# A two-model transformer kernel: latents split earlier and into other tiles, sums of squares one projection later, loop buffers cleared elsewhere, last norm by tokens

## The chip, the cores and the metric

One core of one Trainium2 chip runs the whole program in one launch. The metric is the time on the device, in microseconds (us), as the median of the runs. The engines are called PE (matrix multiplication; its weight loads are listed as PEld), DVE (vector), ACT (activation functions), POOL, and SP, which only issues DMA transfers here.

## The reference, cut to what matters

The input is one sequence of 256 tokens of width 2048, in float32. Three layers follow one another.

1. Layer A: a modulated RMS norm, a wide projection, sparse attention beside a pooled branch, an output projection, and then a mixture of 32 experts. Each token goes to two experts of one group.
2. Layer B ("even"): a norm, a projection, a gated linear recurrence beside sliding-window attention, and an output projection (`wb` in the kernel).
3. Layer C ("odd"): a norm and a projection into latents and differential attention heads; the latents are normed and projected up to queries, keys and values; an output projection (`wc`) and a last norm close it.

```python
def odd_layer(h, w_in, q_norm, w_uq, kv_norm, w_ukv, ..., subln, w_out):
    z = h @ w_in
    c_q, c_kv, k_rope, mla_gate, dq, dk, dv, diff_gate = split_cols(z, ODD_SPLITS)   # c_q is 768 wide, c_kv 512
    q = (rmsnorm_2(c_q, q_norm) @ w_uq).reshape(B, S, MLA_HEADS, MLA_NOPE + MLA_ROPE)
    ...
# after each even and odd layer: x = x + layer(rmsnorm_2(x, gain)); at the end: rmsnorm_2(x, final_norm_gain)
```

## The kernel before

**Layout.** The residual stream `X` lies in SBUF as 16 chunks of 128 features by 256 tokens: features on the partitions, tokens along the row. A norm over features is therefore a sum over partitions, made by PE as a product with a matrix of ones.

**Products in three terms.** Each float32 operand of a projection is split into a rounded high part (type fp32r) and the rest. A projection adds high x high, high x low and low x high. Weights arrive by DMA in half units of 128 x 1024 (`land`). ACT makes the high part `WH` (step `hi`, L1636), DVE the low part `WL` (step `lo`, L1945), and PE multiplies (L1185). Four slots hold `WH` and `WL`, so the `hi` of a half waits until PE has used the half four places back. A projection of one chunk of 128 outputs is two halves of 24 matmuls each.

**Order.** Every engine works through its own list in order, written out beforehand by two functions, `order_a` (layer A up to the routing) and `order_bc` (everything behind the expert loop). `Order.proj` appends the halves of one projection to PE's list, its evacuation to ACT's, and the next weights' `hi` and `lo` to ACT's and DVE's. Steps that follow a projection are put on `lagged` and come one or more projections later. A step waits with `needs(engine, step)` until another engine's counter has passed a step. An engine that waits holds up all that stands behind in its list.

**The routing and the loop.** Layer A ends with the routing: `top`, `place` (slot numbers of the tokens), `before` (a list of expert numbers), `pick` (a one-hot matrix for the first tile of 32 tokens), `list` (the number of tiles and the expert of each, cast to integers for SP), `weights`. Then the first tile's tokens are gathered by PE (L1432), copied by ACT (L1777), turned by PE (L1440) and scaled and shifted by DVE (`inputs`, L2361 and L2365, which make `XG`). A loop over the tiles follows. One tile takes 12 MB of expert weights in 12 slots of `ring`; SP reloads a slot when PE has used it (`w_used`, L1043). The first 12 slots are loaded ahead of the loop (L1030). The vector engine clears the loop's buffers: four of them inside `pick` (L2237 to L2240), and four more behind the routing (L2369 to L2372). `weigh` (L2344 to L2350) makes the scatter weights.

**Behind the loop.** After `wb`, layer C projects `cq` (6 chunks), `ckv` (4), `kr`, `dk`, `dq`, `dv`, `dg` and `mg`. The squares of the last `wb` chunk are added on DVE (`sqsum`, L2109) and summed over the partitions by PE (`ss`, L1291); the norm's factor is applied later to the products. The latents `cq` and `ckv` are split into high and low parts by the steps `ch` (ACT, L1678) and `cl` (DVE, L1969), in ten chunks, after the last `mg` projection, because their target `HH`/`HL` holds the layer's input until then. `silu mg` (L1684) and the evacuations of the up-projections `qr` stand behind them in ACT's list.

**The end.** After the last `wc` chunk: ACT evacuates it, DVE adds it to `X` (L2100), ACT squares, DVE sums (L2109), PE sums over the partitions into all 128 of them (L1291), DVE scales (L1920), ACT takes the root (L1701), DVE the reciprocal of 128 x 256 values (L2152), and DVE multiplies each of the 16 chunks by gain and factor (L2163); SP writes four groups out.

## Time and profile before

| | |
|---|---|
| median of 3 runs | 2349.46 us (2347.33 to 2351.78) |
| profiled execution, its own time | 2358.7 us |
| its span, first to last instruction | 2356.9 us |
| PE busy | 2089.4 us (89%) |
| mean DMA rate | 295 GB/s |

The time of the profiled execution is 1.8 us more than its span and 9.2 us more than the median of the timed runs. The page cuts the span into 40 slices of 58.9 us. Slices 1 to 9 are layer A, 10 to 24 the loop over the tiles, 25 to 40 the layers B and C. In the timeline, a row has its start, the time that it spans, the engine, the line, the operation, what it writes and reads, and behind that in brackets the idle time of the engine before it and what ended it.

### The profile page before, as it was taken

To read this page: it belongs to the slowest core of one execution; us is meant where nothing else is said; L and a number is where in the kernel's file an instruction comes from. 1 tells how busy PE (TensorE), PEld (TensorE's weight loads), DVE (VectorE), ACT (ScalarE), POOL (GpSimd) and SP (SyncE) were. 2 spreads that over 40 slices of the span, in tenths; PEclk is the share of its full clock that TensorE was granted. 3 is DMA by queue.
4 is the path that set the end of the run, shared out by engine and by line. 5 is a ranking of instruction groups with operands and counts; after the bars stand their busy time and mean duration, and the time that the engine had idled before them with its cause. 6 is when DMAs were issued, how large, how long until landed. Compare 5 with 4: busy or idle time off the path is not lost.

```text
span 2356.9 us, 38440 instructions
## 1 busy us (share of the span) xinstructions
PE 2089.4 (89%) x14538; PEld 1364.2 (58%) x14538; DVE 1252.0 (53%) x2281; ACT 858.9 (36%) x1312; POOL 55.2 (2%) x56
## 2 busy tenths in 40 slices
PE   6899998989988888888888888999999999997997
PEld 2677766762222222222222222998889999997887
DVE  3455567545444444444444445558866454577655
ACT  3333344431111111111111113457855444565543
POOL 0000000000000000000000001011100010010000
PEclk9999999999999999999999999999999999998998
DMA  9998987899999999999999999463445455542442
GB/s 368 354 348 291 310 285 233 299 350 364 427 428 428 428 427 427 427 428 428 428 427 427 427 428 372 166 208 121 134 152 182 153 177 182 175 147 88 135 134 91
DMA packets 135047, 695.43 MB, mean 295 GB/s; under 512 B 14992, under 2 KB 15120, under 8 KB 85264
## 3 DMA queue, kind: packets, MB, share of 16 engines
q1 hardware_dynamic: 134928, 693.79, 76.7%
q8 instruction: 81, 1.33, 0.2%
q14 instruction: 38, 0.31, 0.0%
HBM read 691.63 MB, written 2.10 MB: 294 GB/s over the span
## 4 chain that ended last, share of the span: by engine, by line
PE 49%; DMA 34%; DVE 8%; ACT 4%; SPq 3%; issue 2%; DVEq 0%; ACTq 0%
PE acc L1185 34%; DMA ring<-in_w 30%; DMA land<-in_stream_a 3%; PE psO L1237 3%; PE psS L1468 3%; PE acc L1182 3%; DVE WL L1945 2%; SPq L1043 2%; ACT WH L1636 1%; DMA land<-in_stream_bc 1%; PE psM L1454 1%; PE acc L1454 1%; PE psT L1119 1%; ACT SB L1722 0%; PE psO L1127 0%
## 5 line engine op out<-in xcount | busy, mean ns | idle before, releaser
L1185 PE MATMUL acc<-HH,WH 128*128 128x256 f32 x2152 | 633.8, 295 | 11.8 <-DVE HL L1969 5.4
L1945 DVE TENSOR_TENSOR WL<-land,WH 128x1024 fp32r<-128x1024 f32 (+2 forms) x346 | 417.4, 1208 | 417.7 <-ACT WH L1636 413.6
L1185 PE MATMUL acc<-HH,WL 128*128 128x256 f32 x2152 | 616.0, 286 | 0.0
L1185 PE MATMUL acc<-HL,WH 128*128 128x256 f32 x2152 | 615.2, 286 | 0.0
L1636 ACT ACTIVATE WH<-land 128x1024 fp32r<-128x1024 f32 (+2 forms) x350 | 362.4, 1037 | 222.3 <-PE acc L1185 176.8
L1185 PEld LDWEIGHTS acc<-HH,WH 128*128 128x128 f32 x2152 | 420.5, 195 | 34.6 <-issue 11.6
L1185 PEld LDWEIGHTS acc<-HH,WL 128*128 128x128 f32 x2152 | 420.6, 195 | 2.0 <-issue 1.0
L1185 PEld LDWEIGHTS acc<-HL,WH 128*128 128x128 f32 x2152 | 419.9, 195 | 0.0
L1468 PE MATMUL psS<-ring,low 128*32 128x512 f32 x2048 | 273.9, 607 | 105.3 <-DMA ring<-in_w 100.8
L1468 PEld LDWEIGHTS psS<-ring,low 128*32 128x32 f32 x2048 | 40.8, 108 | 316.4 <-DMA ring<-in_w 285.0
L2355 DVE TENSOR_TENSOR X<-acc,X 128x512 f32<-128x512 f32 x128 | 88.6, 692 | 218.9 <-PE acc L1454 218.9
L1787 ACT ACT_TABLE_LOAD x32 | 41.1, 1283 | 447.1 <-PE psS L1468 447.1
L2355 DVE TENSOR_TENSOR X<-psM,X 128x512 f32<-128x512 f32 x128 | 88.6, 692 | 210.0 <-PE psM L1454 210.0
L1492 PE MATMUL psO<-ring,SB 128*32 128x512 f32 x1024 | 122.3, 598 | 42.9 <-DVE SB L2389 35.8
L1454 PE MATMUL psM<-low 128*128 128x512 f32 x264 | 150.4, 652 | 4.9 <-DVE low L2377 2.3
L1454 PE MATMUL acc<-low 128*128 128x512 f32 x264 | 149.3, 647 | 1.4 <-DVE X L2096 1.4
L1787 ACT ACTIVATE low<-psS 128x512 f32<-128x512 f32 x64 | 38.2, 597 | 244.6 <-PE psS L1468 244.2
L1237 PE MATMUL psO<-land,high_a 128*32 128x512 f32 x672 | 96.1, 648 | 35.2 <-DMA land<-in_stream_a 34.4
L1454 PEld LDWEIGHTS psM<-low 128*128 128x128 f32 x264 | 39.7, 189 | 116.6 <-DVE X L2355 80.5
L1454 PEld LDWEIGHTS acc<-low 128*128 128x128 f32 x264 | 39.5, 188 | 112.4 <-DVE X L2355 107.6
L1185 PE MATMUL acc<-lowR,WH 128*128 128x256 f32 x512 | 95.4, 289 | 5.8 <-DVE lowR L1964 5.8
L1492 PEld LDWEIGHTS psO<-ring,SB 128*32 128x32 f32 x1024 | 27.1, 109 | 116.6 <-DVE SB L2389 43.4
(370 smaller groups left out, 2413.4 us busy)
## 6 DMA issues: line engine op xcount, KB each, us to landing
ring<-in_w SPq DMA_DIRECT2D x384, 1024.0 KB, 26.0
land<-in_stream_a SPq DMA_DIRECT2D x284, 512.0 KB, 7.6
land<-in_stream_bc SPq DMA_DIRECT2D x246, 512.0 KB, 4.0
land<-in_stream_bc SPq DMA_DIRECT2D x12, 384.0 KB, 3.5
X<-in_xT SPq DMA_DIRECT2D x1, 2048.0 KB, 14.0
out<-low SPq DMA_DIRECT2D x4, 512.0 KB, 2.6
cst<-in_const SPq DMA_DIRECT2D x1, 1514.5 KB, 9.6
low<-in_w_pool SPq DMA_DIRECT2D x1, 1024.0 KB, 8.3
```

Source lines behind the costliest of these rows:

```text
L1043: sp.dma_start(ring[:, s, :], src[bass.ds(e, 1), s % 4, :, :].rearrange("e p n -> (e p) n")).then_inc(tile_in[s], 16)
L1119: mm = pe.transpose(psT[:, kt, h, :], SB[:, n % 2, h, P * kt:P * kt + P], ident)
L1182: mm = pe.matmul(bank[:, S * tt:S * tt + S], h[rows[kk]][:, P * tt:P * tt + P], w[:, kk, :], start=(z == 0 and i == 0 and tt == 0), stop=s ...
L1185: mm = pe.matmul(bank[:, 0:S], w[:, kk, :], h[rows[kk]], start=(z == 0 and i == 0), stop=stop)
L1237: mm = pe.matmul(bank[CAP * c:CAP * c + CAP, :], cB[:, 4 * q + c, :], w[c // 2][:, c % 2, :], start=(q == 0), stop=(q == 3), tile_position ...
L1454: return pe.matmul(ybank[m % 2], OE[:, P * c:P * c + P], SJ[:, 2 * half:2 * half + 2, :], start=True, stop=True)
L1468: mm = pe.matmul(bH[s // 4][CAP * c:CAP * c + CAP, :], XG[:, k % 4, k // 4, :], ring[:, s, 512 * c:512 * c + 512], start=(s % 4 == 0), sto ...
L1492: mm = pe.matmul(bW2[CAP * c:CAP * c + CAP, :], AT[:, s - 8, :], ring[:, s, 512 * c:512 * c + 512], start=(s == 8), stop=(s == 11), tile_p ...
L1636: ins = act.activation(wh, src, ACT.Copy)
L1787: act.activation(HS[:, b, :], bankS[b], ACT.Copy).then_inc(moe["h_copied"], 1)
L1945: ins = dve.tensor_tensor(wl, src, wh, ALU.subtract)
L2355: dve.tensor_tensor(moe_out(m), ybank[m % 2].rearrange("p (a s) -> p a s", a=2), moe_out(m), ALU.add)\
```

## The change

It has four parts.

1. **Latents.** `ch` and `cl` of the ten latent chunks move from behind `mg` to behind the first ten projections of `dk` and `dq`, one chunk a projection. The high parts go to the columns of tables that no step reads any more (cosines, sines and rotation matrices of layer A, in `cst`) and to free chunks; the low parts overwrite the latents themselves (`latent_split`).
2. **Squares.** `ss` of the last `wb` chunk comes one projection later on PE, and so do the sums of the `cq` chunks.
3. **Start of the loop.** The clears move into two steps, `clear 0` (behind ACT's copy of the gate rows, within the last `wo` projections) and `clear 1` (between `top` and `place`). `pick` comes directly behind `place`, ahead of the list of experts, the gather becomes a step of PE's list, and `weigh` for the first tile comes ahead of `list`. PE's ten filler products become nine. Within the loop `pick` waits for ACT's copy of the gathered tokens (`g_copied`), no longer for PE's gather.
4. **Last norm.** DVE adds the last `wc` chunk straight from PSUM. The sum of squares is taken by tokens (a column of two values a partition, four products on PE), root and reciprocal work on 128 x 2 values, and two products spread the factor over all partitions into PSUM (`rwide`). ACT multiplies each `X` chunk by the gain during the `wc` projections (`gx`, 16 of them), and DVE then multiplies by the factor from PSUM in five operations (`FINAL`).

```diff
+LAST_OUT = ("wc", KD - 1)
+FINAL = ((0, 4), (4, 4), (8, 4), (12, 2), (14, 2))
 def evac_by(x):
-    return "dve" if x[0] in ("bk", "p") else "act"
+    return "dve" if x[0] in ("bk", "p") or x == LAST_OUT else "act"
...
             if x[0] != "wp":
                 self.add("act", "sq", x)
+            if x[0] == "wc":
+                self.add("act", "gx", x[1])
...
-        if x[1] == KD - 1:
+        if x == ("wb", KD - 1):
+            self.lagged.append((1, self.sum_squares, x))
+        elif x[1] == KD - 1 or x == ("wc", KD - 2):
             self.sum_squares(x)
...
             o.add("act", "gt2rows")
+            o.add("dve", "clear", 0)
...
+    o.add("dve", "clear", 1)
     o.add("dve", "place")
     o.add("pe", "keep_busy")
-    o.add("dve", "before")
+    o.add("dve", "pick")
+    o.add("pe", "gather")
     o.add("pe", "beforeT")
     o.misc.append(("beforeT",))
-    o.add("dve", "pick")
+    o.add("dve", "weights")
     o.add("dve", "list")
-    o.add("dve", "weights")
...
         o.proj(("cq", n))
-        o.lagged.append((1, o.sum_squares, ("cq", n)))
+        o.lagged.append((2, o.sum_squares, ("cq", n)))
...
-    for n in range(8):
-        o.proj(("dk", n))
-    for n in range(8):
-        o.proj(("dq", n))
+    latent = [("cq", c) for c in range(6)] + [("ckv", c) for c in range(4)]
+    for x in [(name, n) for name in ("dk", "dq") for n in range(8)]:
+        o.proj(x)
+        if latent:
+            z = latent.pop(0)
+            o.add("act", "ch", *z)
+            o.add("dve", "cl", *z)
...
-    for name, n in (("cq", 6), ("ckv", 4)):
-        for c in range(n):
-            o.add("act", "ch", name, c)
-            o.add("dve", "cl", name, c)
     o.add("act", "silu", "mg", 0, 8)
...
+        def latent_split(name, c):
+
+            hi = {"cq": (0, 1, 2, 3, 60, 61), "ckv": (62, 63, 51, None)}[name][c]
+            hi = rotR[:, :] if hi is None else cosR[:, hi, :] if hi < 4 else highR[:, hi - 48, :]
+            at = (cCQ if name == "cq" else cCKV) + c
+            return hi, lowR[:, at, :] if at < 48 else highR[:, at - 48, :]
...
                 if not first:
-                    dve.wait_ge(moe["g_full"], i)
+                    dve.wait_ge(moe["g_copied"], i)
...
+                    elif what == "gx":
+                        n = step[1]
+                        needs("dve", *(("evac", LAST_OUT) if n == KD - 1 else ("res", ("wc", n))))
+                        ins = act.activation(W(MIX + n)[:, 0, :], X[:, n, :], ACT.Copy, scale=C("gain_f", n, 1))
...
+                        if step[1] == "wc":
+                            then(dve.reciprocal(rtok, rsum))
+                            for tt in range(NT):
+                                ins = dve.tensor_scalar(RT[:, P * tt:P * tt + P], ident, rtok[:, tt:tt + 1], None, ALU.mult)
...
-                        g = C("gain_f")
-                        for c in range(4 * step[1], 4 * step[1] + 4):
-                            ins = dve.scalar_tensor_tensor(out=W(MIX + c)[:, 0, :], in0=X[:, c, :], scalar=g[:, c:c + 1],
-                                                           in1=RT, op0=ALU.mult, op1=ALU.mult)
+                        z = W(MIX + c, n)
+                        ins = dve.tensor_tensor(z, z, psM[:, None, 0:S].to_broadcast([P, n, S]), ALU.mult)
```

**How the instructions move.** Three places follow, rows of the built programs; they hold no times. The first is DVE's list from the end of `place` (the reduction into `small`) to the first operation of the loop. `sti` holds the list for SP, `psO` and `low` are loop buffers. Before:

```order
L2233 TENSOR_REDUCE small<-high_a 128x2 x2
...
L2235 COPY SB<-cst 128x128
...
L1821 TENSOR_TENSOR SB<-SB 128x64
...
L2247 CAST sti<-psM 1x48
L2205 TENSOR_REDUCE high_a<-high_a 128x2
...
L2332 TENSOR_LOAD sti
L2332 ISA x2
L2369 MEMSET psO 128x512
L2370 MEMSET low 128x512
...
L2361 TENSOR_TENSOR low<-acc,small 128x512
L2365 TENSOR_TENSOR low<-low,ada 128x512
```

And after:

```order
L2289 TENSOR_REDUCE small<-high_a 128x2 x2
L1862 TENSOR_SCALAR SB<-SB,small 128x32
...
L1866 TENSOR_TENSOR SB<-SB 128x64
L2305 TENSOR_SCALAR high_a<-high_a,cst 128x32
...
L2410 TENSOR_SCALAR SB<-SB 128x128
L2310 CAST sti<-high_a 1x1
L2311 CAST sti<-psM 1x48
L2421 TENSOR_TENSOR low<-acc,small 128x512
L2425 TENSOR_TENSOR low<-low,ada 128x512
L2432 TENSOR_LOAD sti
```

The five operations of `pick` now stand directly behind `place`, the clears are gone from here, and DVE reads the number of tiles (TENSOR_LOAD) behind `XG` and not ahead of it.

The second place is ACT's list around the last `mg` evacuation (L1596, in the change L1637), with `exp` of a softmax (L1722, L1765) ahead and `silu mg` behind. Before:

```order
L1722 ACTIVATE SB,small<-SB,small 128x256 x4
L1678 ACTIVATE HH_54<-low 128x256 x8
L1678 ACTIVATE HH_54<-high_bc 128x256 x2
L1684 ACT_TABLE_LOAD
L1684 ACTIVATE low<-low 128x2048
```

And after:

```order
L1637 ACTIVATE low<-acc 128x256
L1677 ACTIVATE WH_50<-land_58 128x1024
...
L1765 ACTIVATE SB,small<-SB,small 128x256 x4
L1677 ACTIVATE WH_50<-land_58 128x1024
L1723 ACT_TABLE_LOAD
L1723 ACTIVATE low<-low 128x2048
```

The ten copies of the latents between `exp` and the table load of `silu` are gone from this place.

The third place is the end of DVE's list. Before:

```order
L2100 TENSOR_TENSOR X<-X,high_bc 128x256
L2109 TENSOR_TENSOR high_bc<-high_bc 128x256 x2
L1920 TENSOR_SCALAR high_bc<-psM 128x256
L2152 RECIPROCAL high_bc<-high_bc 128x256
L2163 SCALAR_TENSOR_TENSOR low<-X,col,high_bc 128x256 x16
```

And after:

```order
L2192 TENSOR_TENSOR X<-X,acc 128x256
L2153 TENSOR_TENSOR high_bc<-high_bc 128x256
L2160 TENSOR_SCALAR small<-psM 128x2
L2203 RECIPROCAL small<-small 128x2
L2205 TENSOR_SCALAR high_bc<-cst,small 128x128 x2
L2221 TENSOR_TENSOR low<-low,psM 128x1024 x3
L2221 TENSOR_TENSOR low<-low,psM 128x512 x2
```

The operations on 128 x 256 values between the sum and the last products are replaced by ones on 128 x 2 and 128 x 128, and 16 last products by five larger ones.

## Rows read from the trace of the kernel before

**Rows 1.** The page: the DMA rate of the 40 slices.

```profile
GB/s 368 354 348 291 310 285 233 299 350 364 427 428 428 428 427 427 427 428 428 428 427 427 427 428 372 166 208 121 134 152 182 153 177 182 175 147 88 135 134 91
```

**Rows 2.** Windows: span, busy time of the engines, PE's clock, DMA share, GB/s.

```profile
530.00:535.00 5.00, 2.63 (x9) 0.71 (x10) 3.68 (x11) 0.00 (x0) 0.00 (x0) 0.52 0.12 51
...
620.00:640.00 20.00, 18.32 (x122) 5.40 (x120) 11.23 (x27) 3.06 (x5) 0.00 (x0) 1.00 1.01 428
```

**Rows 3.** Timeline of DVE, from the end of `place` to `XG`.

```profile
522.39 0.24 DVE L2242 TENSOR_SCALAR high_a<-high_a,cst 128x32 f32<-128x32 f32 x1
...
523.15 0.30 DVE L1817 TENSOR_SCALAR SB<-SB,small 128x32 f32<-128x32 f32 x1
...
524.11 0.23 DVE L1821 TENSOR_TENSOR SB<-SB 128x64 f32<-128x64 f32 x1
...
525.00 0.18 DVE L2247 CAST sti<-psM 1x48 int32<-1x48 f32 x1
...
526.02 0.16 DVE L2209 TENSOR_TENSOR small<-small,high_a 128x2 f32<-128x2 f32 x1
527.36 0.48 DVE L2369 MEMSET psO<- 128x512 f32 x1 [1.18 <-issue]
...
529.16 0.17 DVE L2344 TENSOR_SCALAR SB<-SB,small 128x128 f32<-128x128 f32 x1
...
530.72 0.68 DVE L2361 TENSOR_TENSOR low<-acc,small 128x512 f32<-128x512 f32 x1
```

**Rows 4.** Timeline of PE and of SP's queue at the loop's start.

```profile
524.48 1.92 PE L1432 MATMUL acc<-low,SB 128*32 128x512 f32 x16 [0.63 <-DVE SB L1821]
527.17 0.66 PE L1440 MATMUL acc<-cst,low 128*128 128x128 f32 x4 [0.77 <-ACT low L1777]
532.37 1.94 PE L1468 MATMUL psS<-ring,low 128*32 128x512 f32 x8 [4.54 <-DVE low L2365]
...
534.50 26.26 SPq L1043 DMA_DIRECT2D ring<-in_w  x12
```

**Rows 5.** Timeline of DVE and PE around the last squares of `wb`.

```profile
1823.23 1.22 DVE L1945 TENSOR_TENSOR WL<-land,WH 128x1024 fp32r<-128x1024 f32 x1 [0.70 <-ACT WH L1636]
...
1825.06 1.19 PE L1291 MATMUL psM<-high_bc,ones 128*128 128x256 f32 x2 [4.20 <-DVE high_bc L2109]
...
1826.26 0.41 PE L1185 MATMUL acc<-HH,WL 128*128 128x256 f32 x1
...
1833.82 0.59 PE L1291 MATMUL psM<-high_bc,ones 128*128 128x256 f32 x2
```

**Rows 6.** Timeline of ACT, DVE and PE behind the last `mg`.

```profile
2143.16 3.55 ACT L1678 ACTIVATE HH<-low 128x256 fp32r<-128x256 f32 x8
...
2147.62 1.28 ACT L1684 ACT_TABLE_LOAD   x1
...
2152.23 0.96 DVE L1945 TENSOR_TENSOR WL<-land,WH 128x768 fp32r<-128x768 f32 x1 [3.99 <-ACT WH L1636]
...
2156.40 1.11 PE L1119 MATMUL psT<-cst,SB 128*128 128x128 f32 x4 [4.62 <-DVE SB L1893]
```

**Rows 7.** Timeline of ACT, PE and DVE at the end of the program.

```profile
2340.84 0.38 ACT L1578 ACTIVATE high_bc<-acc 128x256 f32<-128x256 f32 x1 [2.97 <-issue]
...
2342.92 1.19 PE L1291 MATMUL psM<-high_bc,ones 128*128 128x256 f32 x2 [2.17 <-DVE high_bc L2109]
...
2345.26 1.75 DVE L2152 RECIPROCAL high_bc<-high_bc 128x256 f32<-128x256 f32 x1 [0.61 <-ACT high_bc L1701]
2347.05 6.80 DVE L2163 SCALAR_TENSOR_TENSOR low<-X,col,high_bc 128x256 f32<-128x256 f32 x16
```

**Rows 8.** Page group of a PSUM-fed DVE addition; ACT's timeline during `dk` and `wc`.

```profile
L2355 DVE TENSOR_TENSOR X<-acc,X 128x512 f32<-128x512 f32 x128 | 88.6, 692 | 218.9 <-PE acc L1454 218.9
...
1912.40 1.06 ACT L1636 ACTIVATE WH<-land 128x1024 fp32r<-128x1024 f32 x1 [1.39 <-PE acc L1185]
...
2320.68 1.06 ACT L1636 ACTIVATE WH<-land 128x1024 fp32r<-128x1024 f32 x1 [0.38 <-PE acc L1185]
```

More of the change, by code:

```diff
@@ L785, in order_bc @@
     o.add("dve", "rstd", "wc")
-    for g in range(4):
+    o.add("pe", "rwide")
+    for g in range(len(FINAL)):
         o.add("dve", "final", g)
@@ L1162, in product @@
                     HH, HL = ([z[:, c, :] for c in range(KD)] for z in (HH0, HL0))
+                elif name in ("qn", "qr", "kn", "vm"):
+                    HH, HL = ([latent_split(*z)[i] for z in [("cq", c) for c in range(6)] + [("ckv", c) for c in range(4)]]
+                              for i in range(2))
                 else:
@@ L1280, in run @@
                                            start=False, stop=True, skip_group_check=True)
+                    elif what == "ss" and step[1][0] == "wc":
+                        x = step[1]
+                        first = x != LAST_OUT
+                        if first:
+                            misc_free(("ssum", "wc"))
+                            needs(k, "dve", o, "sqsum", x)
+                            sq = W(dSA)[:, 0, :]
+                        else:
+                            needs(k, "act", o, "sq", x)
+                            sq = W(dSQ + x[1] % 2)[:, 0, :]
+                        for tt in range(NT):
+                            mm = pe.matmul(psM[:, tt:tt + 1], sq[:, P * tt:P * tt + P], ones[:, 0:1],
+                                           start=(first and tt == 0), stop=not first, skip_group_check=True)
+                    elif what == "rwide":
+                        needs(k, "dve", o, "rstd", "wc")
+                        for tt in range(NT):
+                            mm = pe.matmul(psM[:, P * tt:P * tt + P], ones[:, :], W(dRT)[:, 0, P * tt:P * tt + P], start=True, stop=True)
                     elif what == "ss":
@@ L1374, in run @@
                     elif what == "keep_busy":
-                        for _ in range(10):
+                        for _ in range(9):
                             mm = pe.matmul(bankS[1][:, 0:S], ones[:, :], X[:, 0, :], start=True, stop=True)
+                    elif what == "gather":
+                        needs(k, "act", o, "evac", ("h2t", (1, 3)))
+                        mm = gather(0)
                     elif what == "beforeT":
                         misc_free(step)
-                        needs(k, "dve", o, "before")
+                        needs(k, "dve", o, "pick")
                         mm = pe.matmul(psM[0:1, 0:48], eid[:, 0:1], ident[:, 0:48], start=True, stop=True)
@@ L1773, in copy_gather @@
             def copy_gather(i, first=False):
-                act.wait_ge(moe["g_full"], i + 1)
-                if not first:
+                if first:
+                    act.wait_ge(done[0]["pe"], A.at["pe"][("gather",)])
+                else:
+                    act.wait_ge(moe["g_full"], i)
                     act.wait_ge(moe["gt_full"], i)
@@ L2233, in run @@
                             ins = dve.tensor_reduce(pos_w[:, 2 * kk:2 * kk + 2], tmp2[:, kk], AX.X, ALU.add)
-                    elif what == "pick":
+                    elif what == "clear" and step[1] == 0:
+                        needs("act", "gt2rows")
                         dve.tensor_copy(J, K("slot")).then_inc(moe["j_ready"], 1)
-                        pick(0, True)
                         dve.memset(AT, 0.0).then_inc(moe["at_ready"], 1)
@@ L2327, in run @@
                     count += 1
-            dve.wait_ge(table_in, 32)
-            run(0, A)
-            dve.wait_ge(done[0]["dve"], len(A.steps["dve"]))
-            tiles = dve.value_load(sti[0:1, 48:49], min_val=1, max_val=MAX_TILES)
             OE = W(mOE, 2).rearrange("p a s -> p (a s)")
```

141 lines of the change are left out of this document (79 added, 62 removed).

## The prediction

> **What bounds the kernel now.** First the page's slices [rows 1]: in slices 12 to 24 the DMA rate stands at 427 to 428 GB/s. That is the loop, and its time is the bytes of the expert weights; PE waits there. A change can shorten it only by letting the stream start earlier. In layers A, B and C the rate is far below that, and PE is nearly always busy, so there the waits of PE count one for one. I then listed PE's idle times and read what ended each. Four places touch the change: ahead of the loop [rows 3, 4], at the last squares of `wb` [rows 5], behind the last `mg` [rows 6], and the end [rows 7]. Nothing else in this kernel moves.
>
> **1. Start of the loop.** The first 12 slots are full soon after 530 us: from there to 535 the DMA share is 0.12 [rows 2]. The next transfer is issued at 534.50, when PE's first group of expert products, begun at 532.37, has released a slot [rows 4]. PE waited 4.54 us for `XG` there. The chain after the change, hop by hop:
> - `place` ends just ahead of 522.39, where the list of experts starts; `pick` starts 0.76 us later at 523.15 [rows 3]. It now takes that place, so all of `pick`, gather, copy and turn come 0.76 earlier: the gather at 523.72, the turned tiles at 527.17 + 0.66 - 0.76 = 527.07 [rows 4].
> - What else DVE must have done by then: `pick` 1.19 (523.15 to 524.34), the expert list 0.5 at most (it fits into the 0.76 with a copy of 0.23), `weights` 1.00 (525.18 to 526.18), `weigh` 1.56 (529.16 to 530.72), and the casts 0.3: from 522.39 to 526.94. That is just ahead of 527.07, so neither is much of a wait for the other.
> - `XG` starts at 527.2, and PE 1.65 later (530.72 to 532.37): 528.85. The gain is 532.37 - 528.85 = 3.5 us. The clears (527.36 to 529.16 with the reading of the tile count ahead of them, 1.18) have left this chain [rows 3]. They cost nothing if their new places are idle: seven small operations before the last two `wo` chunks, where I read DVE idle for 4.7 us ahead of the next addition, and two in DVE's wait for PE between `top` and `place`. Without that cover they cost their 1.8 and 0.8 us.
> - The first eight products take 1.94 us after that wait, against about 1.06 in full loop tiles, and the granted clock of the stretch is 0.52, the lower of the two levels (1.2 against 2.4 GHz) [rows 2, 4]. PE's idle time before them shrinks from 4.54 to 1.8 us. If the clock then stays high, the slot is free 0.9 us sooner still: 4.4. I take 3.8; the ends are 0 and 4.4.
>
> The Trainium skill, "TensorE: Matmul & The Clock Gate", section "HAM oscillation", says that waits between bursts of products bring the low clock back, so that each burst starts slow. By that rule a shorter wait is the way to keep it; the sum would be 0.6 us larger. The trace agrees on the slow restart, at 0.52.
>
> **2. Squares.** PE finishes `cq` 0 at about 1820.7 and stands until 1825.06 (4.20 idle), because the addition of the last squares stands on DVE behind a `lo` that ends at 1824.45 [rows 5]. Then `cq` 1 runs at 0.213 us a product instead of 0.12 (0.41 long each instead of 0.28) and is done at 1833.82 [rows 5]. One projection later the sum is ready: `cq` 1 runs straight on, 1820.7 + 48 x 0.12 = 1826.5, and the squares follow in 0.25. The point that was reached at 1833.8 is reached at 1826.7: 7.1 us. The weights for it are there: `WL` for `cq` 2 is complete at 1824.45 [rows 5], and the next `hi` needs only the half that ends at 1823.6. What comes late next: the sum over `cq` 0 must wait for DVE to have read the `wb` sum; that read stands behind two more `lo` and ends at about 1830.6, `cq` 2 at 1832.5. Lower bound 4.2 (the wait alone), upper 7.5.
>
> **3. Latents.** Here the wait named on PE misleads. PE waits 5.4 us for the first latent part, but if that wait alone goes, PE runs one up-projection and a second and then waits for the transposes at 2156.40 [rows 6], and these wait on ACT. The chain: ten latent copies (2143.16 to 2147.61), table load, `silu mg`, evacuation, `hi`, then DVE's `lo` at 2152.23, for which DVE stood 3.99 us [rows 6], then normalising and scaling (4.1 us), then the transposes at 2156.40. Without the ten copies the table load follows `exp` at once, at 2143.16, and every later link comes 2147.62 - 2143.16 = 4.46 us earlier. PE waits at the transposes instead, some 8 us, and restarts there at the low clock as it does now. So the gain is 4.5 and not 5.4 plus the slow products of the first projection. In `dk` and `dq` the ten copies cost ACT 0.44 us a projection, where it has 1.39 idle ahead of its second `hi` alone, and DVE the same, with more [rows 8]. A `hi` ends 2.4 us with its `lo` behind it and is read three halves later (8.6 us). Ends 3.5 and 6.
>
> **4. The end.** Old chain: PE done 2340.75, evacuation, addition, squares, sum, and the last 16 products start at 2347.05 and end at 2353.85 [rows 7]. New chain, from the same instant:
> - DVE adds from PSUM at 2340.87, 0.43; then the sum of the squares of chunk 14 stands on DVE, to 2341.76; four small products on PE for each of two sums, 0.55 each: 2343.0.
> - Three operations on 128 x 2, 0.17 to 0.2 each with 0.1 between engines: 2343.8. Two of 128 x 128 on DVE, 0.5: 2344.35.
> - `rwide` on PE: 0.6 at the high clock, 1.2 at the low one, by the two levels at which the squares ran [rows 5, 7]: 2345.0 to 2345.6.
> - The last products: PSUM-fed 128 x 512 takes 0.69 [rows 8]. Eight of these would be 5.5; three are doubled, and one start saved in each makes it about 5.3. End 2350.6, against 2353.85: 3.2. The 1.75 us of the wide reciprocal [rows 7] are the main part.
> - The last transfer is half as large (256 KB against 512 KB), about 0.6 us at 428 GB/s [rows 1]; I count 0.4.
>
> Together 3.6, ends 2 and 4.5. The 16 `gx` on ACT cost about 0.5 each in `wc`, where ACT's idle time before the second `hi` is 0.38 [rows 8]: that `hi` starts 0.1 late and has 6 us to spare.
>
> The Trainium skill speaks against this part. "VectorE: DVE Perf Modes", section "The TRN2 errata", gives an operation that reads PSUM about twice the fixed cost of one that reads SBUF. By its table, an estimate, the old 16 products would take 5.2 us and the new five 4.9. The trace has 6.80 for the old ones, so the measurement decides.
>
> **Sum.** 3.8 + 7.1 + 4.5 + 3.6 = 19.0 us. Against the profiled execution (2358.7, of them 2356.9 span) that is 2339.7; against the median 2349.46, which is 9.2 below it, 2330.5. The four waits lie on the chain in either, so I forecast 2330.5.
>
> **The rivals.**
> - *Start of the loop gives nothing.* The stream runs until slots run out: if the new order frees the later slots no sooner, or SP's reading of the list (now 1.5 us later) holds the first transfer, only 15.2 remain: 2334.3. For it: from 535 to 560 the rate is still under 428. Against: every slot is released by the same PE list, which shifts as a whole. Chance 0.1.
> - *The squares' wait only moves.* If the `wb` sum is read later than `cq` 2 ends, PE stops one projection later and restarts slowly again. Half of the 7.1 is left: 2334.0. My margin is 1.9 us. Chance 0.08.
> - *PE's first wait was the bound in the latents, and the transposes come early too.* Then 5.4 and the slow products (18 x 0.09) go, 7.0 in all: 2328.0. Against: DVE's 3.99 us wait on ACT [rows 6]. Chance 0.06.
> - *ACT falls behind.* 26 additional operations of 0.5, if none found idle time, give back 13 us: 2343.5. Against: [rows 8]. Chance 0.05.
> - *Slower.* `pick` in the loop now waits for ACT's copy, 0.8 us behind the gather. If DVE were on the chain of each tile, 32 x 0.8 = 25.6 us would be added: 2356.1. It decides once more than 0.6 us a tile gets through. Against: the loop runs at 428 GB/s [rows 1, 2], and that copy belongs to the tile before. Chance 0.02.
> - *No change within 0.2%.* The program does what it says by its order of instructions; only several failures of the above would leave less than 4.7 us. Chance 0.02.
>
> My forecast has the rest, 0.67. 0.2% is 4.7 us, about what a measurement of this kernel can tell from no change. Faster: all but the last two cases and part of the ACT case, 0.95; same 0.03; slower 0.02. The range takes the ends of the parts, not all at one side: 0 to 4.4, 4.2 to 7.5, 3.5 to 6 and 2 to 4.5 give 12.5 to 21 if two fall short, with some room for the spread of medians: 2325.5 to 2337.5. This takes in the first three rivals.
>
> **What would show it.** The first expert product near 528.9 and SP's first reload near 530 to 531; no idle time of PE at the last squares, and `cq` 1 at 0.12 a product; no PE wait ahead of the first `qr`, but one of some 8 us ahead of the transposes of the last differential job, 4.5 us earlier relative to the end of `mg`; the last multiplication some 10 us behind PE's last projection, against 13.1 now. I am wrong if the loop's end moves by less than its start, if PE shows a new wait between `cq` 1 and `ckv`, or if `WH` in `wc` comes late.

## The result, and the profile after

The changed kernel took 2329.29 us (median of 4 runs, 2328.52 to 2330.41), the kernel before 2348.60 (4 runs): 19.3 us less. The ratio is 0.9925, with a 95% interval of 0.9910 to 0.9939, which is 14.3 to 21.1 us. The forecast was 2330.5, of them 19.0 us gained.

Whoever subtracts the two profiled spans gets another number, 2356.9 - 2327.9 = 29.0 us. The profiled execution of before was 9.2 us above its timed runs, and that of the changed kernel 1.1 above its own. So the rows shown ahead of the prediction hold some 9 us that a usual execution does not have. Where they lie is the first experiment.

**Start of the loop.** Timelines of PE, DVE and SP's queue of the changed kernel; they answer to [rows 3, 4].

```profile
519.92 0.30 DVE L1862 TENSOR_SCALAR SB<-SB,small 128x32 f32<-128x32 f32 x1
520.87 0.23 DVE L1866 TENSOR_TENSOR SB<-SB 128x64 f32<-128x64 f32 x1
521.25 1.92 PE L1096 MATMUL acc<-low,SB 128*32 128x512 f32 x16 [0.45 <-DVE SB L1866]
523.94 0.66 PE L1104 MATMUL acc<-cst,low 128*128 128x128 f32 x4 [0.73 <-ACT low L1822]
524.32 0.18 DVE L2311 CAST sti<-psM 1x48 int32<-1x48 f32 x1
524.63 0.69 DVE L2421 TENSOR_TENSOR low<-acc,small 128x512 f32<-128x512 f32 x1
526.28 1.06 PE L1509 MATMUL psS<-ring,low 128*32 128x512 f32 x8 [1.69 <-DVE low L2425]
528.36 1.06 PE L1509 MATMUL psS<-ring,low 128*32 128x512 f32 x8
530.41 1.06 PE L1509 MATMUL psS<-ring,low 128*32 128x512 f32 x8
527.55 31.84 SPq L1065 DMA_DIRECT2D ring<-in_w  x16
```

`pick` starts where `place` ends, `XG` begins at 524.63, right behind the turned tiles (523.94 + 0.66), and PE waits 1.69 us instead of 4.54. The whole profile is 2.5 us earlier here than that of before; *route* in the table below differs by more than that between executions of equal code. Counted from the copy that opens `place` (516.93 now, 519.42 before), the first expert product comes at 9.35 us instead of 12.95: 3.6 earlier, where I had 3.5. The first eight take 1.06 us and not 1.94. SP reloads the first slot 10.62 us after that copy (527.55) and not 15.08 (534.50), 4.5 sooner.

**Squares and latents.** PE's timeline at the last squares of `wb` [rows 5], then DVE, ACT and PE behind the last `mg` [rows 6].

```profile
1816.49 0.28 PE L1250 MATMUL acc<-HL,WH 128*128 128x256 f32 x1
1816.62 0.59 PE L1373 MATMUL psM<-high_bc,ones 128*128 128x256 f32 x2
1819.97 0.42 DVE L2166 TENSOR_SCALAR high_bc<-psM 128x256 f32<-128x256 f32 x1
1822.80 0.59 PE L1373 MATMUL psM<-high_bc,ones 128*128 128x256 f32 x2
...
2126.43 1.28 ACT L1723 ACT_TABLE_LOAD   x1
2131.03 0.96 DVE L1990 TENSOR_TENSOR WL<-land,WH 128x768 fp32r<-128x768 f32 x1 [5.57 <-ACT WH L1677]
2135.20 1.12 PE L1181 MATMUL psT<-cst,SB 128*128 128x128 f32 x4 [7.50 <-DVE SB L1938]
```

The wait ahead of the first up-projection in the kernel before, which has no counterpart now:

```profile
2144.24 0.55 PE L1185 MATMUL acc<-HH,WH 128*128 128x256 f32 x1 [5.44 <-DVE HL L1969]
```

PE goes straight from a projection into the squares, with no idle time. DVE has read the sum of `wb` by 1820.39, 2.4 us before PE overwrites it at 1822.80, so no wait has taken the old one's place. In the latents, the wait of 5.44 us that stood ahead of the first up-projection is gone, and one of 7.50 us stands ahead of the transposes: the forecast had some 8.

**The end.** Timeline of PE, DVE and SP's queue; it answers to [rows 7].

```profile
2316.35 1.02 PE L1357 MATMUL psM<-ones,high_bc 128*128 128x1 f32 x8 [1.13 <-DVE high_bc L2153]
2318.24 0.48 DVE L2205 TENSOR_SCALAR high_bc<-cst,small 128x128 f32<-128x128 f32 x2
2318.78 0.71 PE L1362 MATMUL psM<-high_bc,ones 128*128 128x128 f32 x4 [1.40 <-DVE high_bc L2205]
2319.60 5.17 DVE L2221 TENSOR_TENSOR low<-low,psM 128x1024 f32<-128x1024 f32 x5 [0.87 <-PE psM L1362]
2320.85 4.29 SPq L1072 DMA_DIRECT2D out<-low  x5
```

PE's last projection ended at 2315.22 (2316.35 less the 1.13 idle) and the last multiplication at 2324.77, 9.55 us later; the forecast was 9.9. From there to the end of the span it is 3.13 us, against 3.05 before. The last transfer is half as large, and that gained nothing.

### The profile page after: what moved, and what is told of

Its sections match the earlier page's. It is cut to its first block, busy times and chain, and to the rows that moved or that the text cites. A ratio compares the mean times of both kernels' runs of the same rounds, so it can differ in the third digit from the quotient of the medians.

```text
span 2327.9 us, 38446 instructions
## 1 busy us (share of the span) xinstructions
PE 2076.3 (89%) x14546; PEld 1354.5 (58%) x14546; DVE 1249.1 (54%) x2271; ACT 866.4 (37%) x1327; POOL 55.2 (2%) x56
## 4 chain that ended last, share of the span: by engine, by line
PE 50%; DMA 34%; DVE 7%; ACT 3%; SPq 3%; issue 2%; DVEq 0%; ACTq 0%
PE acc L1250 35%; DMA ring<-in_w 30%; DMA land<-in_stream_a 4%; PE psO L1302 3%; PE acc L1247 3%; PE psS L1509 3%; DVE WL L1990 2%; SPq L1065 2%; ACT WH L1677 1%; DMA land<-in_stream_bc 1%; PE acc L1118 1%; PE psM L1118 1%; PE psT L1181 1%; PE psO L1195 0%; PE psO L1189 0%
## 5 line engine op out<-in xcount | busy, mean ns | idle before, releaser
L1250 PE MATMUL acc<-HH,WH 128*128 128x256 f32 x2048 | 598.6, 292 | 6.4 <-DVE HL L2009 4.1
L1250 PE MATMUL acc<-HH,WL 128*128 128x256 f32 x2048 | 583.2, 285 | 0.0
L1250 PE MATMUL acc<-HL,WH 128*128 128x256 f32 x2048 | 583.0, 285 | 0.0
L1250 PEld LDWEIGHTS acc<-HH,WH 128*128 128x128 f32 x2048 | 397.0, 194 | 28.0 <-issue 11.6
L1250 PEld LDWEIGHTS acc<-HH,WL 128*128 128x128 f32 x2048 | 397.1, 194 | 1.7 <-issue 1.0
L1250 PEld LDWEIGHTS acc<-HL,WH 128*128 128x128 f32 x2048 | 396.6, 194 | 0.0
L1250 PE MATMUL acc<-lowR,WH 128*128 128x256 f32 x600 | 119.8, 287 | 5.8 <-DVE lowR L2009 5.8
L1250 PEld LDWEIGHTS acc<-lowR,WH 128*128 128x128 f32 x600 | 98.2, 194 | 6.8 <-ACT lowR L1712 4.3
```

The costliest lines, as they stand in the source:

```text
L1250: mm = pe.matmul(bank[:, 0:S], w[:, kk, :], h[rows[kk]], start=(z == 0 and i == 0), stop=stop)
```

## The experiments

All kernels of a group ran beside the kernel before. The summary over all 14 profiles comes first, since each experiment draws on it. Each profile is cut at the same events; the stretches are differences of start times, in us:

- *route*: to the copy that opens `place`. *loop*: from there to the first transfer of the weights behind the loop. *B*: to the last product of `cq` 0. *sq*: to the first product of `cq` 2. *C1*: to the second of the four long reciprocals (128x512) of layer C. *lat*: to the third. *r*: to the fourth. *C2*: to the end of the last projection. *tail*: to the end of the last multiplication.

```
                     route    loop      B     sq     C1    lat      r     C2   tail
before              519.42  917.13 384.03  13.48 294.04  29.27  23.39 159.99  13.10
before_again        517.32  916.81 380.69  12.57 294.04  29.27  21.17 158.15  12.57
only_squares        520.46  917.02 383.79   6.12 294.52  29.27  22.68 156.52  12.58
only_latents        519.46  916.50 380.47  12.57 294.05  24.80  23.42 158.14  12.57
only_start          521.84  912.71 381.38  12.56 294.05  29.28  21.18 156.37  12.57
only_norm           515.54  917.02 383.37  12.51 294.04  29.27  21.18 155.04   9.56
the changed kernel  516.93  910.31 383.50   6.12 294.52  24.80  21.14 157.90   9.55
after_again         517.77  911.72 383.30   6.12 294.53  24.79  21.15 157.84   9.55
after_no_squares    512.33  911.46 381.50  12.53 294.05  24.79  22.68 157.75  10.08
after_fill          518.85  911.07 383.54   6.12 294.52  24.79  21.16 157.70  10.06
after_silu          515.92  914.49 383.52   6.13 294.51  21.58  21.16 161.35   9.56
after_silu_dve      519.29  910.85 383.22   6.13 294.52  19.73  23.44 158.08   9.64
after_reorder       513.46  913.02 383.69   6.12 294.52  20.50  23.67 158.39   9.55
after_reorder_fill  515.12  912.07 381.16   6.13 294.52  20.51  23.66 160.27   9.56
```

Three columns are nearly constant wherever the code is the same (*sq*, *C1*, *lat*), and four move by 2 to 10 us between executions of equal code (*route*, *B*, *r*, *C2*). What is read from the first kind is exact to tenths, but for the *sq* of the first profile of before; a whole time is not.

### before_again: where the surplus of the first profile lies

The kernel before, without an edit.

> The kernel before, unchanged: a control, and a second profile of it. The profiled execution of before took 2358.7 us, 9.2 us more than its timed runs; that of the changed kernel took 2330.4, 1.1 more than the median of its runs. Theory 1 (chance of the execution): the surplus sits in stretches that ran at a low PE clock behind a wait, 2170 to 2180 us with a granted clock of 0.70 and 0.62 above all, and a second profile shows another set of them, so its span comes out between 2345 and 2352. Theory 2 (the recording itself costs it): the second profile has again a span near 2357 and the same slow stretches. Ratio to before 1.000 in either.

Measured: 1.0002 (0.9989 to 1.0016), its span 2345.6. Theory 1 holds, with a span inside its 2345 to 2352: the second profile is 11.3 us shorter, by 2.1 in *route*, 3.3 in *B*, 0.9 in *sq*, 2.2 in *r*, 1.8 in *C2* and 0.5 in *tail*. What differs is PE's clock, wherever it was looked up: in *sq* and *r* below, in the tail, and at one place in *B* (see what stays open). *route*, *C2* and the rest of *B* were not traced to it. A window in the stretch *r* and PE's row at its wait, first of the first profile and then, the same place 6.7 us earlier, of the second; the number ahead of the DMA share is the granted clock.

```profile
2170.00:2180.00 10.00, 8.36 (x38) 7.36 (x39) 3.66 (x7) 2.67 (x4) 0.00 (x0) 0.66 0.22 74
2172.76 1.22 PE L1335 MATMUL psM<-high_bc,cst 128*128 128x256 f32 x2 [1.53 <-DVE high_bc L2315]
```

```profile
2163.30:2173.30 10.00, 8.34 (x60) 7.46 (x61) 5.84 (x8) 4.20 (x6) 0.00 (x0) 1.00 0.28 85
2166.09 0.70 PE L1335 MATMUL psM<-high_bc,cst 128*128 128x256 f32 x2 [1.53 <-DVE high_bc L2315]
```

The wait is 1.53 us in both, but around it one execution ran at 0.66 and the other at full speed, and the same two products took 1.22 and 0.70. The tail shows it in one row: the sum of the last squares [rows 7] takes 1.19 us in the first profile, and in the second this.

```profile
2332.19 0.67 PE L1291 MATMUL psM<-high_bc,ones 128*128 128x256 f32 x2 [2.17 <-DVE high_bc L2109]
```

1.19 - 0.67 = 0.52 is the whole difference of the two tails (13.10 and 12.57). After a wait of 2.17 us in both, the products came out at either level.

### only_squares and after_no_squares: the second part alone, and left out

The first is before with these lines, the second the changed kernel without them:

```diff
-        if x[1] == KD - 1:
+        if x == ("wb", KD - 1):
+            self.lagged.append((1, self.sum_squares, x))
+        elif x[1] == KD - 1:
...
-        o.lagged.append((1, o.sum_squares, ("cq", n)))
-        if n == 0:
+        o.lagged.append((2, o.sum_squares, ("cq", n)))
+        if n == 1:
```

> Before with the second part of the change alone: the squares of the last wb chunk and those of the cq chunks come one projection later. My step: the wait of 4.20 us and the slow cq 1 behind it go, 7.1 us in all, about 2341.5, with cq 1 at 0.12 us a product. Rival 1, the wait alone goes and the products stay slow: 4.2 us. Rival 2, the wait moves one projection on: 3.6 us, with a new idle time of PE ahead of the sum over cq 0.

> The changed kernel with the second part undone (the squares of the last wb chunk one projection earlier again). From cq 0's last product to the first of cq 2 it took 13.48 us in the first profile of before, 12.57 in the second, and 6.13 in the changed kernel. Theory: undone, it costs 6.4 us, near 2337. Rival 1 (the parts alone and together differ, since a wait of 4.2 us is a place where something else can catch up): less than 5. Rival 2 (my own 7.1): only where the low clock lasts as long as in the first profile.

Measured: 0.9976 (0.9960 to 0.9992), 5.6 us, for the part alone. Without it the changed kernel stood at 0.9946 (0.9933 to 0.9958) where it has 0.9925 and 0.9926 in two measurements: 4.8 us. In the stretch *sq* it is sharp: 6.12 or 6.13 in all eight profiles with the part and 12.51 to 12.57 in five of the six without it; only the first profile of before had 13.48. The difference is 6.4, and 0.48 comes back in *C1* (294.52 against 294.04), where the two products of the sum over `cq` 0 now lie, so 6.0. The wait and the slow restart both go, as in my step, so it is not the wait alone (rival 1 of the first expectation); rival 2 is out too, since none of the eight profiles with the part has a new wait: PE's first idle time behind these squares is one of 0.40 us, 26 us on, and the kernels without the part have the same one with 0.36. The 4.8 us of the timed runs lie under the 5 that rival 1 of the second expectation set, but their interval does not tell 4.8 from 6.0; the stretch does. My 7.1 was taken from the one execution in which the low clock lasted longest. Windows of before_again show the shorter dip behind the same wait:

```profile
1814.00:1819.00 5.00, 1.10 (x10) 0.89 (x8) 4.19 (x5) 2.59 (x4) 0.00 (x0) 1.00 0.53 178
1819.00:1824.00 5.00, 4.64 (x24) 4.55 (x25) 0.93 (x3) 0.42 (x1) 0.00 (x0) 0.66 0.50 162
```

### only_latents: the first part alone

The edit is that of the diff shown ahead: `ch` and `cl` go behind the projections of `dk` and `dq`, with `latent_split`.

> Before with the first part of the change alone: the ten latent chunks are split behind the first ten projections of dk and dq. My step: the chain over ACT gives 4.5 us, about 2344.1. Rival: 7.0 to 7.4 us, about 2341.5. The two profiles speak for both: between the last mg and the transposes of the last differential job the changed kernel gained 4.47 us, and between there and the first queries of the next jobs another 2.9, because before ran 10 us there at a granted clock of 0.70 and 0.62 and the changed kernel at 1.00. If those 2.9 belong to the change, the profile here shows 1.00 in that stretch and the time falls by 7.4; if they are chance of one execution, timed runs show 4.5.

Measured: 0.9982 (0.9970 to 0.9993), 4.2 us. The stretch *lat* is 24.80 against 29.27: 4.47, and my step had 4.46. The rival's other 2.9 us were chance: *r* is 23.42 here, as long as in the first profile of before. *C1*, in which the ten splits now lie, is 294.05 against 294.04. They cost nothing there.

### only_start: the third part alone

The edits of the diff ahead in `order_a`, `pick`, `clear`, the gather step and the wait on `g_copied`; nothing behind the loop.

> Before with the third part of the change alone: the start of the loop. My step: 3.8 us, of them 3.5 on the chain to XG, about 2344.8. Rival (clock): the two profiles show 6.9 us between the first load of the ring and the end of the loop: 3.7 up to the first expert product, and the rest because the first expert products, the first two additional products behind them and the second eight run at the high clock instead of 0.52 and 0.80; then about 2341.7. Rival (ACT in the loop): if the copy that pick now waits for counted, the time would be 2370 or so, 0.8 us a tile more.

Measured: 0.9979 (0.9965 to 0.9993), 4.9 us. In *loop*, five profiles without the part have 916.50 to 917.13, seven with it and without a filler 910.31 to 914.49, in the mean 912.1: 4.8 us, in single executions 2.4 to 6.6. ACT's copy is on no chain in the loop, or *loop* would be 25 longer. Most of why the gain varies is seen in PE's timelines: first the start alone, then after_again, both with the wait of 1.69 us that the changed kernel has.

```profile
531.18 1.94 PE L1469 MATMUL psS<-ring,low 128*32 128x512 f32 x8 [1.69 <-DVE low L2371]
533.04 1.76 PE L1098 MATMUL psM<-low 128*128 128x512 f32 x2
534.74 1.07 PE L1469 MATMUL psS<-ring,low 128*32 128x512 f32 x8
```

```profile
527.11 1.93 PE L1509 MATMUL psS<-ring,low 128*32 128x512 f32 x8 [1.69 <-DVE low L2425]
528.98 1.71 PE L1118 MATMUL psM<-low 128*128 128x512 f32 x2
530.62 1.06 PE L1509 MATMUL psS<-ring,low 128*32 128x512 f32 x8
```

The same wait, and the first eight products take 1.94 and 1.93 here but 1.06 in the changed kernel's first profile. The second group of eight starts 3.5 or 3.6 us behind the first there, and 2.1 in the changed kernel: 1.5 us lost. In before, 4.54 us of idle time stood ahead, and the third group was slow to start as well:

```profile
536.24 1.42 PE L1468 MATMUL psS<-ring,low 128*32 128x512 f32 x8
538.64 1.06 PE L1468 MATMUL psS<-ring,low 128*32 128x512 f32 x8
```

538.64 is 6.27 us behind the first product at 532.37 [rows 4]; in the changed kernel it is 4.13 (526.28 to 530.41). Read so in all twelve profiles without a filler, *loop* falls into three pieces. From the copy that opens `place` to the first expert product it is 12.93 to 13.04 us in the five without the part and 9.34 or 9.35 in the seven with it: 3.6. From there to the third group it is 6.27 to 6.85 in the five, and in the seven 4.13 three times, 5.56, 5.61, 5.70 and 7.04 (after_silu, where the second group ran slow as well): in the mean 6.6 against 5.2, so 1.4. The rest is 896.8 to 898.1 in all twelve. So the clock behind the wait makes up to 2.9 us of the spread, and 1.3 are of that rest.

### after_fill: filler products in that wait

```diff
             gather_t(0)
+            for _ in range(7):
+                pe.matmul(bankS[1][:, 0:S], ones[:, :], X[:, 0, :], start=True, stop=True)
             needs(0, "dve", A, "list")
```

> The changed kernel with seven filler products (128x256, about 0.22 us each at the high clock, 1.6 us in all) on PE between the turning of the gathered tokens and the first expert product, where PE waits 1.69 us. So far the first expert products ran at the low clock in two of four profiles with that wait (1.93 us for the first eight) and at the high one in the two others (1.06). Theory (PE's idle time ahead of the products decides): with 0.1 us of idle left they run at 1.06 in every execution, and the time is 1 to 1.5 us below after_again in the mean, with a smaller spread. Rival: the clock falls for another reason (the waits of 0.4 and 0.7 us ahead of it, or the light load of the filler itself); then the filler runs at half speed too, ends 1.5 us late, and the time is 1 to 1.5 us above.

Measured: 0.9931 (0.9918 to 0.9944), not below the changed kernel's 0.9925. Timeline of PE:

```profile
526.34 3.19 PE L1501 MATMUL psS<-X,ones 128*128 128x256 f32 x14
529.46 1.07 PE L1511 MATMUL psS<-ring,low 128*32 128x512 f32 x8
```

I had mispriced the filler. The trace writes two rows for one such product, so that 0.22 us is half of one: seven took 3.19 us at the high clock and not 1.6, and put the first expert product 1.3 us late. The products behind it did run at the high clock, here and in after_reorder_fill, but that the filler was the reason is not shown, since without it some executions have it too.

### only_norm: the fourth part alone

The edits of the diff ahead in `evac_by`, `FINAL`, `gx`, the token sums, `rstd`, `rwide` and `final`.

> Before with the fourth part of the change alone: the last norm by tokens. My step: 3.6 us. By the profiles of before: the last multiplication ended 13.10 us after PE's last projection in the first profile, but 12.57 in the second and in those of three single parts; in the changed kernel it ended 9.55 after. So I now expect 3.0 us, about 2345.3, and 9.55 in the profile here. Rival (smaller last transfer counts too): 0.4 us more between the last multiplication and the end of the span; the profiles of before and after speak against it with 3.05 and 3.13 there. Rival (ACT falls behind by gx): the projections of wc take longer than in before, and nothing is gained.

Measured: 0.9986 (0.9969 to 1.0003), 3.3 us, with an interval that reaches no change. The profile decides: *tail* is 9.56 against 12.57 or 12.58 in four profiles without the part, 3.0 us. (The 10.06 and 10.08 of two other kernels are `rwide` at the low clock, 1.22 us in after_fill instead of 0.71.) *C2*, in which the 15 first `gx` run on ACT, is 155.04, no longer than elsewhere.

### after_again: do the parts add up?

The changed kernel, without an edit.

> The changed kernel, unchanged: a second profile and more timed runs. The parts alone gave 0.9976 (squares), 0.9982 (latents), 0.9979 (start of the loop), each with an interval of about 0.0015 to either side. Theory: the parts lie on one chain and add up, with 3.0 us for the norm about 17 to 19 us, ratio 0.992 to 0.993. Rival: they overlap, and the sum is smaller than that. In its profile the wait ahead of the first expert product is again 1.69 us; whether the products behind it run at the high clock, as in the first profile, or at the low one, as in that of the start alone, is open: if it is chance of one execution, either can come.

Measured: 0.9926 (0.9909 to 0.9942), 17.4 us. The four parts alone gave 5.6, 4.2, 4.9 and 3.3, together 18.0. They add up, but each of the four has an interval of 3 to 4 us to either side, so that alone would not show it. The stretches do: *sq*, *lat* and *tail* have the same length with a part alone and with all four (6.12, 24.80 and 24.79, 9.56 and 9.55), and *loop* lies in one spread. By the stretches it is 4.8 + 6.0 + 4.5 + 3.0 = 18.3 us. Its first expert products ran at the low clock, unlike those of the first profile: chance of one execution.

### after_silu, after_silu_dve, after_reorder, after_reorder_fill: the wait that is left

These go at the 7.50 us ahead of the transposes. after_silu takes `silu mg` out of ACT's chain, and after_silu_dve also lets DVE scale ahead of one `lo`:

```diff
-    o.add("act", "silu", "mg", 0, 8)
     for u in (4, 5, 0, 1):
         q_up(u)
+        if u == 0:
+            o.add("act", "silu", "mg", 0, 8)
...
+    d = o.steps["dve"]
+    to = d.index(("scale", ("d", 3, 1)))
+    lo = max(i for i in range(to) if d[i][0] == "lo")
+    d.insert(to, d.pop(lo))
```

> The changed kernel with silu mg (table load and activation, 3.2 us on ACT) taken out of the chain between the last exponentials of the differential jobs and the transposes, and put behind the last square root (dsqrt 3). Theory (the chain over ACT sets the transposes, and PE's wait is only where it shows): evacuation, hi, lo, normalising and scaling all come 3.2 us earlier, PE's wait of 7.50 us becomes 4.2, and the time falls by 3.2 to 3.4 us against after_again. Rival (the wait moves on): DVE, with two additional halves and the reciprocal of 128x512 close behind, holds PE at the next rotation instead, and less than 1 us is left.

> As after_silu, and DVE normalises and scales the last differential job ahead of the lo that stood before them in its list, so that nothing of DVE's work for the transposes waits for ACT's hi. Theory: the transposes come 5.5 to 6.7 us earlier than in the changed kernel, with 1 us of waiting left ahead of them, and 4 to 6 us of it reach the end. Rival: the lo is now late, PE waits for it or for the rotation two projections later, and the gain is that of after_silu or less.

Measured: 0.9927 (0.9909 to 0.9944) and 0.9910 (0.9894 to 0.9927). The first moved the transposes by just what the theory said: *lat* 21.58 against 24.79, 3.2 us, and the timed runs show no gain. Rows of PE and ACT of after_silu show both halves, the wait that became shorter and one that is new:

```profile
2135.18 0.66 PE L1182 MATMUL psT<-cst,SB 128*128 128x128 f32 x4 [4.29 <-DVE SB L1939]
...
2157.93 1.91 ACT L1724 ACTIVATE low<-low 128x2048 f32<-128x2048 f32 x1
2159.87 0.38 ACT L1654 ACTIVATE low<-acc 128x256 f32<-128x256 f32 x1
2160.30 0.39 PE L1251 MATMUL acc<-highR,WH 128*128 128x256 f32 x1 [1.67 <-ACT low L1654]
```

The evacuation at L1654 stands behind `silu mg` in its new place, and with the slow start behind the wait that gives some 2.1 of the 3.2 us back (counted from the second reciprocal, PE is 3.3 us earlier than in after_again ahead of this wait and 1.2 us earlier behind it). That cost is not DVE's, as the rival had it, but ACT's own. *C2* is longer by more than this (161.35 against 157.84), but the other 1.5 us lie 50 us further on, behind a wait that is the same in both (1.87 and 1.85 us). First after_silu, then after_again:

```profile
2211.12 0.41 PE L1251 MATMUL acc<-HH,WL 128*128 128x256 f32 x1
```

```profile
2210.99 0.28 PE L1250 MATMUL acc<-HH,WL 128*128 128x256 f32 x1
```

That is the clock of one execution. So by the stretches after_silu keeps 1.1 us, less than the intervals can show. after_silu_dve brought the transposes 6.5 us forward, as expected, with 0.96 us of waiting left, and *lat* to 19.73, 5.1 us less; it gave 2.3 back in *r*, with a wait of 4.43 us at a rotation. *lat*, *r* and *C2* together are 2.5 us shorter than in after_again, not the 4 to 6 that I expected; by the timed runs it is 3.8 us below after_again, but the two intervals overlap.

after_reorder keeps the DVE move of after_silu_dve, puts `silu mg` behind `kv_up(1)` and moves one rotation ahead of the long reciprocal, and the last kernel adds the filler:

```diff
+    d.remove(("rot", ("qr", 0)))
+    d.insert(d.index(("dfin", 2)), ("rot", ("qr", 0)))
```

> The changed kernel with three moves behind the last mg: silu mg behind the last of the first key and value projections, where ACT stood 2.79 us; the scaling of the last differential job on DVE ahead of one lo; the rotation of qr 0 on DVE ahead of the normalising that begins with the reciprocal of 3.35 us. In after_silu_dve the transposes came 5.1 us earlier, but the first rotation (wait of 4.43 us) took back 2.3 of it, and silu in its place there another 2.1. Theory (each of these waits is one of order on ACT and DVE): 5.1 + 1 to 2 us of gain against the changed kernel, near 2325. Rival: the next reciprocal of 3.35 us, behind dsqrt 3, is on the chain of PE's list anyway and holds the end of the rotations where it was; then the gain is that of after_silu_dve, 3 to 3.8.

> after_reorder and the seven filler products of after_fill together. Theory: the two are independent and add, 6 to 8 us below the changed kernel, 2322 to 2325. Rival (see after_fill): the filler loses 1 to 1.5, and it is slower than after_reorder.

Measured: 0.9921 (0.9905 to 0.9936) and 0.9909 (0.9895 to 0.9923). *lat* and *r* together are 44.17 in both (20.50 + 23.67, 20.51 + 23.66), against 45.94 in after_again and 43.17 in after_silu_dve. Rows of DVE and PE of after_reorder:

```profile
2130.85 0.43 DVE L2079 TENSOR_TENSOR high_bc<-high_bc 128x256 f32<-128x256 f32 x1
2131.31 3.35 DVE L2392 RECIPROCAL high_bc<-high_bc 128x512 f32<-128x512 f32 x1
...
2138.46 0.42 DVE L2079 TENSOR_TENSOR high_bc<-high_bc 128x256 f32<-128x256 f32 x1
...
2138.94 1.22 PE L1424 MATMUL psM<-high_bc,cst 128*128 128x256 f32 x2 [4.11 <-DVE high_bc L2079]
```

The rotation of `qr` 0 is early, at 2130.85, and PE now waits as long for the next one, which stands behind the same reciprocal. This is the rival in another form: the 3.35 us of the reciprocal are still on PE's chain, now ahead of the second rotation, with the normalising, a `lo` and a copy behind them. Whether they leave the chain with both rotations ahead of them was not run. The gains that I expected, to near 2325 and to 2322 to 2325, did not come. No version tried here is shown to beat the changed kernel. The two lowest, 0.9909 and 0.9910, are 3.5 to 4 us below it by these ratios, and the intervals overlap.

## Why the prediction was right, step by step

- **What bounds the kernel.** Each wait that I named was removed for what it held up, and the parts added up (18.0 us alone, 17.4 and 17.6 together by the timed ratios, 18.3 by the stretches). The four places lie on one chain.
- **Start of the loop: 3.8 forecast, 4.8 measured.** The chain to `XG` was right to 0.1 us (3.6 against 3.5). Mis-sized was the term for the clock, "the slot is free 0.9 us sooner": it counted the first eight products alone, but the low clock also holds the two additional products and the next eight (by 2.1 us up to the third group). Measured, it is 1.4 us in the mean where I had put 0.3. It is also not one number: with the same wait of 1.69 us, executions came out at either level, and the gain at 2.4 to 6.6.
- **Squares: 7.1 forecast, 6.0 measured.** Right in mechanism, wait and slow restart. The term was read from an execution with 13.24 us between the last product of `cq` 0 and the next sum, and the five other profiles without the part have 0.9 to 1.0 less. I had also left out the 0.48 that comes back.
- **Latents: 4.5 forecast, 4.47 measured.** The rule that the named wait (5.44 us, on the first latent) was not the one to count, but the four-step chain over ACT behind it, was right to 0.01 us. The rival of 7.0 is out.
- **The end: 3.6 forecast, 3.0 measured.** The new tail was 9.55 where I had 9.9. The old one was 13.10 in the profile that I had and 12.57 in every other: again one low-clock restart. The 0.4 for the smaller last transfer is wrong; it gained nothing.
- **The step from one profile to the median.** I set the gain off against the median although the profile was 9.2 us above it, with the words that the four waits lie on the chain in either. They do, but some 1.4 us of their price were of that one execution (0.9 in *sq*, 0.5 in the tail). The errors, +1.0, -1.1, 0.0 and -0.6, nearly cancel: that the sum of 19.0 came within 1 us of the 18.3 is partly luck, and the sum was better than its terms. The absolute 2330.5 also leaned on a median of three runs of before, 2349.46, that became 2348.60 with a fourth.
- **The rivals.** That the loop's start gives nothing, that the squares' wait moves on, that ACT falls behind, and the in-loop wait on ACT's copy are all out by the columns *loop*, *sq*, *C1* and *C2*.

What I cited from the Trainium skill: "TensorE: Matmul & The Clock Gate", section "HAM oscillation", says that waits between bursts of products bring the low clock back; I drew from it that a shorter wait keeps the high one. The trace agrees only in part, since the same 1.69 us of wait left the clock high for the first eight products in three of seven profiles (1.06 or 1.07 us) and low in three (1.93 or 1.94); one lies between (1.72). And by the table of the Trainium skill, "VectorE: DVE Perf Modes", section "The TRN2 errata", my estimate for the five new products was 4.9 us; the trace has 5.17.

What stays open: *B* is 383.2 to 383.8 in seven of the eight profiles with the squares part and 380.5 to 381.5 in four of the six others. The traces place at least 1.4 us of the difference 91 us ahead of the first instruction that the part moves, behind a wait of 2.34 to 2.37 us that all fourteen have. Behind it the products came at the low clock in nine profiles and at the high one in five, and from there to the end of *B* it is 91.2 to 92.1 us in the nine and 89.7 or 89.8 in the five. The second product behind the wait, first of before_again, then of after_again:

```profile
1725.29 0.28 PE L1185 MATMUL acc<-lowR,WL 128*128 128x256 f32 x1
```

```profile
1721.97 0.42 PE L1250 MATMUL acc<-lowR,WL 128*128 128x256 f32 x1
```

The nine are not only kernels with the part: the first profile of before and only_norm are among them, and after_reorder_fill, which has the part, is not. PE, DVE and ACT work through the same instructions in the same order up to `cq` 0 with the part and without it. So nothing in the traces ties the 1.3 us between the two means to the part; that it is chance is likely, and no run was made to show it.

## What to carry to other kernels

When an engine waits, ask what ended the wait next to it, and price the chain over the other engines and not the idle time: here 5.4 us of idle was worth 4.5, and 7.5 us of idle, attacked in four ways, 4 at most and none of it clear of the noise, since each wait had another one close behind. One profile is one execution: profile the kernel before twice, and take only what both show, above all behind waits of PE. Compare stretches between fixed events and not whole times; where PE's clock is the same in both they resolve 0.1 us, and the intervals of timed runs are 3 to 4 us to either side.

## What was not expected of the hardware

- After equal idle times PE's granted clock came out differently from one execution to the next: 1.06 or 1.93 us for the same eight products behind 1.69 us, 0.67 or 1.19 us for the same sum behind 2.17. The two profiles of before are 11.3 us apart; the four places looked into (in *B*, *sq*, *r* and the tail) all differ in this.
- Five multiplications that read the factor from PSUM, 128 x 4096 values in all, took 5.17 us; 16 with both operands in SBUF [rows 7] took 6.80.
- The end of the span came 3.13 us behind the last multiplication with a last transfer of 256 KB and 3.05 with one of 512 KB.
